# Two of the four chunks of the first layer's feed-forward output as seven products for eight

## The chip, the cores and the metric

The kernel runs on one core of a Trainium2 chip. The metric is the device time of one execution in microseconds, lower is better. TensorE (PE) multiplies, VectorE (DVE) and ScalarE (ACT) work elementwise, GpSimd (POOL) and SyncE (SP) issue transfers. All data is float32.

## The reference

A stack of two layers over 512 tokens (256 of a context, 256 of a latent stream), followed by a second block. The stage of this case is the end of layer 0, whose last part is a gated feed-forward network. D_MODEL is 1024, D_FF is 2816:

```python
def _swiglu(h, w_in, w_out):
    a, b = jnp.split(h @ w_in, 2, axis=-1)
    return (jax.nn.silu(a) * b) @ w_out

xl = xl + ml[5] * _swiglu(_modulate(_rmsnorm(xl, norm_g[l, 1]), ml[3], ml[4]), w_ffn_in[l], w_ffn_out[l])
xc = xc + mc[5] * _swiglu(_modulate(_rmsnorm(xc, norm_g[l, 1]), mc[3], mc[4]), w_ffn_in[l], w_ffn_out[l])
```

The change concerns the last product, with `w_ffn_out` (2816 x 1024). Beside it `w_ada` is multiplied with a condition vector for later layers.

## The kernel before

Activations stand transposed: features on the 128 partitions, the 512 tokens along a row, context in columns 0 to 255 (part 0), latents in 256 to 511 (part 1). `ffn` (in the tile `branches`) holds the 22 feature tiles between the two feed-forward products, `c.x` (`stream`) the residual stream in 8 tiles. The function `tail_of_all` is one stage of the program, ended by a barrier; each engine has its own list of instructions, and semaphores order them.

**Folded products.** The gates, the branches and most up products of this stage (`folded_product`, L1590) use seven multiplications of blocks for eight. A chunk of 256 output features times pairs of input tiles is seen as 2 x 2 blocks, and the two token halves likewise; VectorE forms four sums of weight blocks (`mix_weights`, L1721 to L1724) and four of token blocks (`mix_tokens`), TensorE runs seven products into four banks, ScalarE copies the first, and VectorE puts the results together (`unfold`, L1737 to L1745). The same bank group is used again two products later.

**Down products.** They are plain (`product`, L1566). `down_steps` lists six steps of (chunk, first part, end part); a chunk is 256 output features, so two banks (`half`). Chunks 0 and 1 are made for both parts at once (512 columns), chunks 2 and 3 for part 0 and then again for part 1, so that the norm of part 0 can begin early. The 22 feature tiles come in three weight transfers (`cuts`) of 8, 8 and 6 tiles into a ring of four slots (`weight_ring`, SP, L1554), each released when its products are done (`slot_used`, `product`). VectorE's `add` (L1779) adds a finished bank to `c.x` and counts `drained`; ScalarE squares (L1872, `squared`), TensorE sums the squares over features with a matrix of ones (`sums`, L1627, two steps behind the products), and `average`, `root`, `scale` and `shift` make the normed input of layer 1. `fetch` (L342) loads that layer's first four `w_in` chunks into the same ring.

**Work between.** `condition(n)` lets VectorE do n tiles of the modulation product: each is one 128x1024 operation (L417) on a 512 KB tile that GpSimd loads (L388) into one of two slots, as soon as VectorE has used the one before in it. VectorE's list is fixed by hand:

```python
for s in range(len(down_steps)):
    if s < 2:
        condition(12 if s == 0 else 9)
    add(down_steps, s, P_DOWN, D_DOWN, B_DOWN, 5 * KT)
```

TensorE's banks for it are `B_DOWN + t` modulo 8, so steps 0 to 3 use four different pairs, and only the steps of part 1 wait for `drained`.

Of the kernel before, what the change touches and what calls it, by code (L numbers as in the profile page):

```python
# [1412 lines left out]
def tail_of_all(c, a, w_in, besides, following):  # L1413
# [37 lines left out]
    folded = merges + feeds  # L1451
# [7 lines left out]
    down_steps = [(0, 0, 2), (1, 0, 2), (2, 0, 1), (3, 0, 1), (2, 1, 2), (3, 1, 2)]  # L1459
# [16 lines left out]
    B_OUT, B_SUMS, B_UP, B_DOWN = 0, KT, KT + 2, 4  # L1476
    B_SUMS_2 = B_DOWN + KT
# [42 lines left out]
    with c.stage() as block:  # L1520
        @block.sync
        def _(sp):
# [5 lines left out]
            def wait_used(n):  # L1528
# [9 lines left out]
                elif n < W_DOWN:  # L1538
                    sp.wait_ge(c.folded_product, 4 * (n - weight_of(len(merges)) + len(merges) + 1))
                else:  # L1540
                    s, _, cut = down[n - W_DOWN]
                    if cut == len(cuts) - 1:
                        sp.wait_ge(c.product, P_DOWN + 2 * (s + 1))
                    else:
                        sp.wait_ge(c.slot_used, s * (len(cuts) - 1) + cut + 1)
# [13 lines left out]
        def _(pe):  # L1559
# [60 lines left out]

            def sums(steps, s, base, i):
# [48 lines left out]
            for n in range(len(merges), len(folded)):  # L1670
                folded_product(n)

            for s, (chunk, p0, p1) in enumerate(down_steps):
                for cut, (k0, nk) in enumerate(cuts):
                    w = weights(W_DOWN + s * len(cuts) + cut)
                    for half in range(2):
                        t = 2 * chunk + half
                        if cut == 0 and p0 == 0:
                            pe.wait_ge(c.folded_read, 4 * (len(folded) - (2 if t < 4 else 1) + 1))
                        elif cut == 0:  # L1680
                            pe.wait_ge(c.drained, D_DOWN + evacuations(down_steps, step_of(down_steps, chunk, 0)))
# [8 lines left out]
                if s:  # L1690
                    sums(down_steps, s - 1, wide * KT, B_SUMS_2)
# [3 lines left out]
        def _(dve):  # L1695
# [7 lines left out]
            def mix_tokens(source, out):  # L1703
# [8 lines left out]
                dve.sem_inc(c.tokens_mixed, 1)  # L1712

# [57 lines left out]
            def add(steps, s, base, first, i, gate_tile):  # L1771

                chunk, p0, p1 = steps[s]
                for half in range(2):
                    t = 2 * chunk + half
                    dve.wait_ge(c.product, base + 2 * s + half + 1)
                    for p in range(p0, p1):
                        out = c.x[:, t, cols(p, p + 1)]
                        dve.scalar_tensor_tensor(out, bank(i + t)[:, cols(p, p + 1)],  # L1779
                                                 mod[:, gate_tile + t, parts[p][2]:parts[p][2] + 1], out, ALU.mult, ALU.add  # L1780
                                                 ).then_inc(c.drained, 1)
# [1757 lines left out]
```

## Time and profile before

| | |
|---|---|
| median of 3 runs | 3318.43 us (3316.75 to 3320.65) |
| the profiled execution | 3313.01 us |
| its span, first to last instruction | 3310.9 us |
| mean granted TensorE clock | 0.985 of full speed |
| TensorE, VectorE, ScalarE busy | 92%, 50%, 23% of the span |

Times in rows are us from the start of the span. In a timeline a row merges like instructions in a row; what stands in brackets is idle time before it and what ended it. A float32 product of the program stands in the trace as two matmul records, so an `x` count of 176 is 88 products.

### The profile page before, as it was taken

What the parts mean: (1) busy time and instruction counts of PE and PEld (TensorE: products, weight loads), DVE (VectorE), ACT (ScalarE), POOL (GpSimd) and SP (SyncE); (2) the same over time, 40 slices, a digit from 0 to 9 for tenths busy, and PEclk for the clock granted to TensorE, in tenths of its full rate; (3) what the DMA queues carried; (4) which work ended last, traced back from release to release, by engine and by line L of the source; (5) the groups of instructions that cost most, each with busy time, mean ns of one, the idle gap of its engine ahead of it and who ended that gap; (6) DMA issues with size and microseconds to landing.
All of it is one profiled execution on the core that took longest, in us unless ns stands there. A gap on an engine that the chain in (4) does not pass through costs nothing. (4 is left out here: it accounts for less than half of the span.)

```text
span 3310.9 us, 33325 instructions
## 1 busy us (share of the span) xinstructions
PE 3061.8 (92%) x12426; PEld 2120.6 (64%) x12426; DVE 1652.8 (50%) x3666; ACT 770.0 (23%) x1787; POOL 337.1 (10%) x371
## 2 busy tenths in 40 slices
PE   6999999999999999998999989999988899877776
PEld 2556555758888888485776678878877754322222
DVE  4333444357773676313234437644037377777774
ACT  2222133321001100012111330010023244444443
POOL 0000000000000000100000000000000044444442
PEclk8999999999999999999999999999989999999999
DMA  6221111134442454642322224478431499999997
GB/s 231 83 66 55 51 51 51 51 120 147 127 134 70 141 159 130 197 143 77 102 77 64 64 77 152 152 274 315 143 118 65 142 417 421 421 421 421 420 418 308
DMA packets 280767, 585.87 MB, mean 177 GB/s; under 512 B 11736, under 2 KB 231768, under 8 KB 244256
## 3 DMA queue, kind: packets, MB, share of 16 engines
q0 software_dynamic: 51936, 343.17, 26.3%
q1 hardware_dynamic: 228672, 240.58, 22.5%
q8 instruction: 100, 1.64, 0.2%
q14 instruction: 59, 0.48, 0.0%
HBM read 582.63 MB, written 1.08 MB: 176 GB/s over the span
## 5 line engine op out<-in xcount | busy, mean ns | idle before, releaser
L773 PE MATMUL banks<-normed,weight_ring 128*128 128x512 f32 (+1 forms) x1280 | 487.6, 536 | 29.7 <-PEq L308 18.4
L773 PEld LDWEIGHTS banks<-normed,weight_ring 128*128 128x128 f32 x1280 | 244.7, 193 | 251.5 <-issue 240.0
L782 PE MATMUL banks<-weight_ring,normed 128*128 128x256 f32 x1408 | 319.3, 383 | 4.6 <-DVE work L1263 4.6
L3365 PE MATMUL banks<-weight_ring,work 128*128 128x512 f32 x512 | 248.1, 612 | 60.1 <-ACT work L3265 59.3
L3365 PE MATMUL banks<-work 128*128 128x512 f32 x512 | 253.6, 618 | 53.6 <-ACT work L3265 49.3
L782 PEld LDWEIGHTS banks<-weight_ring,normed 128*128 128x128 f32 x1408 | 265.4, 191 | 58.9 <-issue 23.9
L417 DVE CUSTOM_DVE_ANT_0 work<-work 128x1024 f32<-128x1024 f32 x188 | 223.2, 1223 | 126.1 <-DMA work<-ada_turned 106.4
L2029 PE MATMUL banks<-normed,weight_ring 128*128 128x256 f32 x1088 | 242.4, 386 | 10.6 <-DMA weight_ring<-w_ffn_in 4.0
L2029 PEld LDWEIGHTS banks<-normed,weight_ring 128*128 128x128 f32 x1088 | 210.8, 194 | 41.6 <-DMA weight_ring<-w_ffn_in 4.8
L3365 PEld LDWEIGHTS banks<-weight_ring,work 128*128 128x128 f32 x512 | 88.8, 189 | 198.9 <-ACT work L3265 134.1
L3365 PEld LDWEIGHTS banks<-work 128*128 128x128 f32 x512 | 88.4, 190 | 198.3 <-ACT work L3265 131.6
L1566 PE MATMUL banks<-branches,weight_ring 128*128 128x256 f32 (+1 forms) x656 | 207.5, 478 | 3.4 <-PEq L308 3.4
L3170 DVE CUSTOM_DVE_ANT_0 work<-work,branches 128x1024 f32<-128x1024 f32 x128 | 156.9, 1225 | 95.5 <-DMA work<-experts,branches 94.1
L3170 DVE CUSTOM_DVE_ANT_0 weight_ring<-weight_ring,branches 128x1024 f32<-128x1024 f32 x128 | 156.7, 1225 | 89.8 <-DMA weight_ring<-experts,branches 88.8
L1566 PEld LDWEIGHTS banks<-branches,weight_ring 128*128 128x128 f32 x656 | 124.6, 190 | 84.6 <-issue 75.5
L1590 PE MATMUL banks<-work 128*128 128x256 f32 x744 | 165.6, 379 | 0.0
L3147 POOL DMA_INDIRECT weight_ring<-experts,branches x128 | 141.6, 1107 | 180.6 <-PE banks L3365 174.3
L2029 PE MATMUL banks<-branches,weight_ring 128*128 128x256 f32 x736 | 159.8, 379 | 0.0
L3147 POOL DMA_INDIRECT work<-experts,branches x128 | 134.7, 1053 | 244.0 <-PE banks L3365 170.6
L1590 PEld LDWEIGHTS banks<-work 128*128 128x128 f32 x744 | 141.4, 190 | 19.2
L2029 PEld LDWEIGHTS banks<-branches,weight_ring 128*128 128x128 f32 x736 | 139.8, 190 | 19.0
L1289 DVE TENSOR_REDUCE work<-banks 128x2 f32<-128x1024 f32 (+1 forms) x48 | 50.2, 1046 | 200.3 <-PE banks L885 200.3
(492 smaller groups left out, 3920.4 us busy)
## 6 DMA issues: line engine op xcount, KB each, us to landing
weight_ring<-w_in SPq DMA_DIRECT2D x98, 1024.0 KB, 5.2
weight_ring<-w_ffn_in SPq DMA_DIRECT2D x44, 1024.0 KB, 5.2
work<-ada_turned POOLq DMA_DIRECT2D x80, 512.0 KB, 3.8
work<-ada_turned POOLq DMA_DIRECT2D x18, 1536.0 KB, 9.7
weight_ring<-w_ffn_out SPq DMA_DIRECT2D x20, 1024.0 KB, 5.2
weight_ring<-w_out SPq DMA_DIRECT2D x12, 1024.0 KB, 5.1
weight_ring<-w_br_ml SPq DMA_DIRECT2D x8, 1024.0 KB, 5.1
weight_ring<-w_br_da SPq DMA_DIRECT2D x8, 1024.0 KB, 5.2
```

The lines of the kernel that those rows point to most:

```text
L417: last = dve.tensor_tensor_reduce(out=out, in0=slot[:, t, :], in1=self.rows[:, row, :], scale=1.0, scalar=0.0, op0=ALU.mult, op1=ALU.add, ...
L773: last = pe.matmul(proj_bank(tile)[:, since:T], w[:, kk, half * P:(half + 1) * P], c.h[:, kk, since:T], start=kk == 0, stop=kk == KT - 1)
L782: last = pe.matmul(proj_bank(tile)[:, x * CHUNK:(x + 1) * CHUNK], c.h[:, kk, j * P:(j + 1) * P], w[:, kk, :], start=kk == 0, stop=kk == KT ...
L1289: chain(dve.reduce_max(its[:, 6:8], c.psum[:, u:u + 2, 0:keys(i)], AX.X))
L1566: ins = pe.matmul(bank(i)[:, cols(p0, p1)], w[:, k - at, half * P:(half + 1) * P], source[:, k, cols(p0, p1)], start=k == 0, stop=k == tot ...
L1590: last = pe.matmul(out[:, half * NCTX:(half + 1) * NCTX], left(k), right(k), start=k == 0, stop=k == KT // 2 - 1)
L2029: ins = pe.matmul(bank(i)[:, 0:NLAT], w[:, k - at, half * P:(half + 1) * P], source[:, k, lat], start=k == 0, stop=k == total - 1)
L3147: pool.indirect_dma_start(out=fetched[e % R], out_offset=None, in_=a["experts"], in_offset=bass.IndirectOffsetOnAxis(ap=experts_u[:, e:e + ...
L3170: dve.tensor_tensor_reduce(out=urows[e % R], in0=urows[e % R], in1=tokens[:, t, :], scale=1.0, scalar=0.0, op0=ALU.mult, op1=ALU.add, accu ...
L3365: last = pe.matmul(c.banks[2 * t + half][:], diag[:, r, :], vrows[r][:, half * 512:(half + 1) * 512], start=e == t * H * K, stop=e == (t + ...
```

## The change

Chunks 1 and 2 of the down product become folded, over both parts at once. `down_steps` has five steps: chunk 0, chunks 1 and 2 (both folded), chunk 3 part 0, chunk 3 part 1. A folded step (`folded_down`) runs seven products of 11 tile pairs with 256 columns. Its weight sums are formed for each of the three transfers (`mix_down`) and wait in `down_sums`; all three transfers must be in the ring before the step's first product. The sums of the features (`mix_features`) are made for the 11 pairs of `ffn`: four pairs inside the loop of up products, seven behind it. `add_down` replaces `add`; the squares of steps 0 and 1 go to other tiles, and their sums by TensorE are made behind step 3. Step 0 uses banks 6 and 7, step 1 banks 4 to 7, step 2 banks 0 to 3.

```diff
+    downs = [("down", 0, 1), ("down", 0, 2)]
+    folded = merges + feeds + downs
+    FIRST_DOWN = len(merges) + len(feeds)
...
-    down_steps = [(0, 0, 2), (1, 0, 2), (2, 0, 1), (3, 0, 1), (2, 1, 2), (3, 1, 2)]
+    down_steps = [(0, 0, 2), (1, 0, 2), (2, 0, 2), (3, 0, 1), (3, 1, 2)]
+    mixed_features = ([c.mg[:, 2 * i:2 * i + 2, :] for i in range(4)] + [c.h[:, 2 * i:2 * i + 2, :] for i in range(4)]
+                      + [token_sums[:, i] for i in range(3)])
+    mixed_features = [(v if i >= 8 else v.rearrange("p a (b t) -> p (a b) t", b=2)) for i, v in enumerate(mixed_features)]
+    last_sums = [c.work[:, SUMS_AT + 3072:SUMS_AT + 3840], c.big[:, 22:24, :].rearrange("p k t -> p (k t)")[:, 0:768]]
+    down_sums = [[weight_sums[:, i, x] for x in range(4)] for i in range(2)]
+    down_sums.append([last_sums[x // 2].rearrange("p (s k m) -> p s k m", s=2, m=P)[:, x % 2] for x in range(4)])
+    held_squares = {0: gates[1].rearrange("p (k t) -> p k t", t=T), 1: gates[0].rearrange("p (k t) -> p k t", t=T)}
+    def squares_of(step, t, down):
+        return held_squares[step][:, t % 2] if down and step in held_squares else c.h[:, t]
+    def down_bank(t, part):
+        return (6 + t) if t < 2 else (4 + t % 2 - 4 * part)
...
                     s, _, cut = down[n - W_DOWN]
-                    if cut == len(cuts) - 1:
-                        sp.wait_ge(c.product, P_DOWN + 2 * (s + 1))
+                    if s in (1, 2):
+                        sp.wait_ge(c.weights_mixed, FIRST_DOWN + s)
+                        sp.wait_ge(c.slot_used, s + 2)
+                    elif cut == len(cuts) - 1:
+                        sp.wait_ge(c.product, P_DOWN + 2 * (s + 1 if s == 0 else s - 1))
                     else:
-                        sp.wait_ge(c.slot_used, s * (len(cuts) - 1) + cut + 1)
+                        sp.wait_ge(c.slot_used, cut + 1 + (2 * s - 2 if s else 0))
...
+            def folded_down(s):
+                n, chunk = FIRST_DOWN + s - 1, s
+                slots = [weights(W_DOWN + s * len(cuts) + cut) for cut in range(len(cuts))]
+                first, second, third, fourth = (c.banks[4 * (n % 2) + i] for i in range(4))
+                def their(inputs, outputs):
+                    return lambda k: part_of(slots[k // 4], inputs, outputs)[:, k % 4]
+                def mixture(i):
+                    return lambda k: down_sums[k // 4][i][:, k % 4]
+                def tokens(inputs, half):
+                    return lambda k: quarter(ffn, 2 * k + inputs, half)
+                def token_mixture(i):
+                    return lambda k: mixed_features[k][:, i]
+                def one(out, half, left, right):
+                    for k in range(NF // 2):
+                        last = pe.matmul(out[:, half * NCTX:(half + 1) * NCTX], left(k), right(k), start=k == 0, stop=k == NF // 2 - 1)
+                    return last
+                pe.wait_ge(c.folded_copied, n - 1)
+                one(first, 0, their(0, 0), tokens(0, 0)).then_inc(c.folded_product, 1)
+                pe.wait_ge(c.folded_read, 4 * (n - 2) + 4)
+                one(second, 0, their(1, 0), tokens(1, 0))
+                pe.wait_ge(c.tokens_mixed, 9)
+                if s == 1:
+                    pe.wait_ge(c.drained, D_DOWN + evacuations(down_steps, 0))
+                one(fourth, 1, their(1, 1), token_mixture(3)).then_inc(c.slot_used, 1)
+                pe.wait_ge(c.weights_mixed, n + 1)
+                one(second, 1, mixture(1), token_mixture(1)).then_inc(c.folded_product, 1)
+                one(third, 0, mixture(0), token_mixture(0))
+                one(third, 1, mixture(2), token_mixture(2)).then_inc(c.folded_product, 1)
+                one(fourth, 0, mixture(3), tokens(1, 1)).then_inc(c.folded_product, 1)
...
                 chunk, p0, p1 = steps[s]
                 pe.wait_ge(c.squared, base + evacuations(steps, s))
                 for p in range(p0, p1):
                     for t in (2 * chunk, 2 * chunk + 1):
-                        ins = pe.matmul(bank(i + p)[:, cols(p, p + 1)], c.constant("ones"), c.h[:, t, cols(p, p + 1)],
-                                        start=t == 0, stop=t == KT - 1)
+                        ins = pe.matmul(bank(i + p)[:, cols(p, p + 1)], c.constant("ones"),
+                                        squares_of(s, t, steps is down_steps)[:, cols(p, p + 1)], start=t == 0, stop=t == KT - 1)
...
             for s, (chunk, p0, p1) in enumerate(down_steps):
+                if s in (1, 2):
+                    folded_down(s)
+                    continue
                 for cut, (k0, nk) in enumerate(cuts):
                     w = weights(W_DOWN + s * len(cuts) + cut)
                     for half in range(2):
                         t = 2 * chunk + half
-                        if cut == 0 and p0 == 0:
-                            pe.wait_ge(c.folded_read, 4 * (len(folded) - (2 if t < 4 else 1) + 1))
-                        elif cut == 0:
-                            pe.wait_ge(c.drained, D_DOWN + evacuations(down_steps, step_of(down_steps, chunk, 0)))
+                        if cut == 0:
+                            pe.wait_ge(c.folded_read, 4 * (FIRST_DOWN - 1 if s == 0 else FIRST_DOWN + s - 2))
                         for k in range(k0, k0 + nk):
                             if s == 0 and half == 0 and k % 2 == 0:
                                 pe.wait_ge(c.fed, k // 2 + 1)
-                            last = product(B_DOWN + t, w, half, ffn, p0, p1, (k,), k0, NF)
+                            last = product(down_bank(t, p0), w, half, ffn, p0, p1, (k,), k0, NF)
                         if cut == len(cuts) - 1:
                             last.then_inc(c.product, 1)
                     if cut < len(cuts) - 1:
                         last.then_inc(c.slot_used, 1)
-                if s:
-                    sums(down_steps, s - 1, wide * KT, B_SUMS_2)
+                    if s == 4 and cut == 0:
+                        sums(down_steps, 3, wide * KT, B_SUMS_2)
+                if s == 3:
+                    pe.wait_ge(c.folded_read, 4 * len(folded))
+                    for done in range(3):
+                        sums(down_steps, done, wide * KT, B_SUMS_2)
             sums(down_steps, len(down_steps) - 1, wide * KT, B_SUMS_2)
...
+            def mix_features(pairs):
+                for i in pairs:
+                    out, b = mixed_features[i], ffn[:, 2 * i:2 * i + 2, :].rearrange("p two (h t) -> p two h t", h=2)
+                    chain(dve.tensor_tensor(out[:, 0], b[:, 0, 1], b[:, 0, 0], ALU.subtract))
+                    chain.mark(dve.tensor_tensor(out[:, 2], b[:, 1, 1], b[:, 0, 1], ALU.subtract))
+                    chain(dve.tensor_tensor(out[:, 1], b[:, 1, 1], out[:, 0], ALU.subtract))
+                    chain.mark(dve.tensor_tensor(out[:, 3], b[:, 1, 0], out[:, 1], ALU.subtract))
+                chain.wait()
+                dve.sem_inc(c.tokens_mixed, 1)
+            def mix_down(s, cut):
+                n, (_, nk) = W_DOWN + s * len(cuts) + cut, cuts[cut]
+                wait_weights(dve, n)
+                w = c.ring[:, n % SLOTS, 0:nk, :]
+                if s == 2:
+                    dve.wait_ge(c.folded_product, 4 * (FIRST_DOWN + 1))
+                out = down_sums[cut]
+                chain.mark(dve.tensor_tensor(out[0], part_of(w, 0, 1), part_of(w, 1, 1), ALU.add))
+                chain(dve.tensor_tensor(out[2], part_of(w, 0, 0), part_of(w, 0, 1), ALU.subtract))
+                chain(dve.tensor_tensor(out[1], out[0], part_of(w, 0, 0), ALU.subtract))
+                chain(dve.tensor_tensor(out[3], part_of(w, 1, 0), out[1], ALU.subtract))
+                if cut == len(cuts) - 1:
+                    dve.sem_inc(c.weights_mixed, 1)
...
+            def add_down(s):
+                chunk, p0, p1 = down_steps[s]
+                if s in (1, 2):
+                    unfold(FIRST_DOWN + s - 1)
+                    dve.wait_ge(c.folded_read, 4 * (FIRST_DOWN + s))
+                for half in range(2):
+                    t = 2 * chunk + half
+                    if s not in (1, 2):
+                        dve.wait_ge(c.product, P_DOWN + 2 * (s if s == 0 else s - 2) + half + 1)
+                    for p in range(p0, p1):
+                        out = c.x[:, t, cols(p, p + 1)]
+                        source = spare.rearrange("p (k t) -> p k t", t=T)[:, half] if s in (1, 2) else c.banks[down_bank(t, p0)]
+                        dve.scalar_tensor_tensor(out, source[:, cols(p, p + 1)], mod[:, 5 * KT + t, p:p + 1], out, ALU.mult, ALU.add
...
-            for n in range(len(merges), len(folded)):
+            for n in range(len(merges), FIRST_DOWN):
                 _, i, chunk = folded[n]
-                if n + 1 < len(folded):
+                if n + 1 < FIRST_DOWN:
                     mix_weights(n + 1)
+                if i and 1 <= chunk <= 4:
+                    mix_features((chunk - 1,))
                 condition(2 if i == 0 else 1)
                 unfold(n)
                 if i:
                     feed(n, chunk)
             scales(mod_next, KT, c.vector("norm_g", 2 * KT, 3 * KT))
-            for s in range(len(down_steps)):
-                if s < 2:
-                    condition(12 if s == 0 else 9)
-                add(down_steps, s, P_DOWN, D_DOWN, B_DOWN, 5 * KT)
-                if s == len(down_steps) - 2:
-                    average(0, 3, B_SUMS_2)
-                    scale(0, 3)
+            dve.wait_ge(c.folded_product, 4 * FIRST_DOWN)
+            mix_features(range(4, NF // 2))
+            condition(12)
+            for cut in range(2):
+                mix_down(1, cut)
+            add_down(0)
+            mix_down(1, 2)
+            condition(9)
+            add_down(1)
+            for cut in range(3):
+                mix_down(2, cut)
+            for s in (2, 3):
+                add_down(s)
+            average(0, 3, B_SUMS_2)
+            scale(0, 3)
+            add_down(4)
...
             for s in range(len(down_steps)):
+                if s in (1, 2):
+                    copy_first(FIRST_DOWN + s - 1)
```

TensorE at steps 0 and 1, before: the last rows of step 0 (chunk 0), all of step 1 (chunk 1, from the row that waits for `loaded1` on), and the first sums.

```order
L1566 MATMUL banks<-branches,weight_ring 128x512 [waits fed]
L1566 MATMUL banks<-branches,weight_ring 128x512 x7
L1566 MATMUL banks<-branches,weight_ring 128x512 [waits folded_read,loaded1]
L1566 MATMUL banks<-branches,weight_ring 128x512 x7
L1566 MATMUL banks<-branches,weight_ring 128x512 [waits folded_read]
L1566 MATMUL banks<-branches,weight_ring 128x512 x7
L1566 MATMUL banks<-branches,weight_ring 128x512 [waits loaded2]
L1566 MATMUL banks<-branches,weight_ring 128x512 x15
L1566 MATMUL banks<-branches,weight_ring 128x512 [waits loaded3]
L1566 MATMUL banks<-branches,weight_ring 128x512 x11
L1627 MATMUL banks<-normed,constants_sb 128x256 [waits squared]
```

After the change, step 1 from its first product to the fourth:

```order
L1661 MATMUL banks<-branches,weight_ring 128x256 [waits loaded3,folded_copied,loaded2,loaded1]
L1661 MATMUL banks<-branches,weight_ring 128x256 x10
L1661 MATMUL banks<-branches,weight_ring 128x256 [waits folded_read]
L1661 MATMUL banks<-branches,weight_ring 128x256 x10
L1661 MATMUL banks<-merged,weight_ring 128x256 [waits drained,tokens_mixed]
L1661 MATMUL banks<-merged,weight_ring 128x256 x3
L1661 MATMUL banks<-normed,weight_ring 128x256 x4
L1661 MATMUL banks<-work,weight_ring 128x256 x3
L1661 MATMUL banks<-merged,work 128x256 [waits weights_mixed]
L1661 MATMUL banks<-merged,work 128x256 x3
```

The plain step of 44 products waited for weights and for free banks that had been read long before. The folded step waits ahead of its third product (22 products in) for `drained`, the adds of step 0, and for the sums of the features, and 11 products later for the sums of its own weights.

VectorE ahead of the first `add`, before: the last of the 12 tiles, the four adds of step 0, and the first of the 9 tiles.

```order
L417 ISA work,modulation<-work 128x1024 [waits ada_summed,ada_loaded0]
L417 ISA modulation 128x1
L1779 SCALAR_TENSOR_TENSOR stream<-banks,modulation,stream 128x256 [waits ada_summed,product]
L1779 SCALAR_TENSOR_TENSOR stream<-banks,modulation,stream 128x256
L1779 SCALAR_TENSOR_TENSOR stream<-banks,modulation,stream 128x256 [waits product]
L1779 SCALAR_TENSOR_TENSOR stream<-banks,modulation,stream 128x256
L417 ISA work,modulation<-work 128x1024 [waits ada_summed,ada_loaded1]
L417 ISA modulation 128x1
```

After the change, from the last of the 12 tiles on (L1795 to L1798 are `mix_down`, L1884 is `add_down`):

```order
L417 ISA work,modulation<-work 128x1024 [waits ada_summed,ada_loaded0]
L417 ISA modulation 128x1
L1795 TENSOR_TENSOR work<-weight_ring 128x512 [waits ada_summed,loaded1]
L1796 TENSOR_TENSOR work<-weight_ring 128x512
L1797 TENSOR_TENSOR work<-work,weight_ring 128x512 [waits vec_done]
L1798 TENSOR_TENSOR work<-weight_ring,work 128x512 [waits vec_done]
L1795 TENSOR_TENSOR work<-weight_ring 128x512 [waits loaded2,vec_done]
L1796 TENSOR_TENSOR work<-weight_ring 128x512
L1797 TENSOR_TENSOR work<-work,weight_ring 128x512 [waits vec_done]
L1798 TENSOR_TENSOR work<-weight_ring,work 128x512 [waits vec_done]
L1884 SCALAR_TENSOR_TENSOR stream<-banks,modulation,stream 128x256 [waits product,vec_done]
L1884 SCALAR_TENSOR_TENSOR stream<-banks,modulation,stream 128x256
```

The twelve tiles, in front of these rows in both, are now behind 28 operations of `mix_features`, of which these are the last pair's, with the first tile:

```order
L1780 TENSOR_TENSOR work<-branches 128x256
L1781 TENSOR_TENSOR work<-branches 128x256 [waits vec_done]
L1782 TENSOR_TENSOR work<-branches,work 128x256
L1783 TENSOR_TENSOR work<-branches,work 128x256 [waits vec_done]
L417 ISA work,modulation<-work 128x1024 [waits vec_done,ada_summed,ada_loaded1]
L417 ISA modulation 128x1
```

Before, only the two operations of `scales` stood between the end of the feed and the first tile. And eight operations on weights now stand between the last of the 12 tiles and the adds that TensorE waits for.

## Rows read from the trace of the kernel before

**Rows 1.** The page: span, busy time, share and instructions of two engines.

```profile
span 3310.9 us, 33325 instructions
...
PE 3061.8 (92%) x12426; PEld 2120.6 (64%) x12426; DVE 1652.8 (50%) x3666; ACT 770.0 (23%) x1787; POOL 337.1 (10%) x371
```

**Rows 2.** Busy time in a stretch: engines, granted clock, DMA share, GB/s.

```profile
1345.00:1360.00 15.00, 15.00 (x36) 6.65 (x35) 6.16 (x10) 0.00 (x0) 2.13 (x5) 1.00 0.76 243
```

**Rows 3.** Timeline of TensorE, 1320 to 1491: start, length, instruction, count.

```profile
1320.12 3.62 PE L1590 MATMUL banks<-normed,weight_ring 128*128 128x256 f32 x16
...
1332.20 75.70 PE L1566 MATMUL banks<-branches,weight_ring 128*128 128x512 f32 x176
1407.74 1.89 PE L1627 MATMUL banks<-normed,constants_sb 128*128 128x256 f32 x8
1409.46 19.16 PE L1566 MATMUL banks<-branches,weight_ring 128*128 128x256 f32 x88
1428.46 1.89 PE L1627 MATMUL banks<-normed,constants_sb 128*128 128x256 f32 x8
...
1488.89 1.03 PE L1627 MATMUL banks<-normed,constants_sb 128*128 128x256 f32 x4
1490.08 1.13 PE L1627 MATMUL banks<-normed,constants_sb 128*128 128x256 f32 x4 [0.16 <-ACT normed L1872]
```

**Rows 4.** Timeline of VectorE, 1334 to 1370.

```profile
1334.79 1.22 DVE L417 CUSTOM_DVE_ANT_0 work<-work 128x1024 f32<-128x1024 f32 x1
...
1340.12 1.23 DVE L417 CUSTOM_DVE_ANT_0 work<-work 128x1024 f32<-128x1024 f32 x1 [2.61 <-DMA work<-ada_turned]
...
1345.37 1.22 DVE L417 CUSTOM_DVE_ANT_0 work<-work 128x1024 f32<-128x1024 f32 x1 [1.76 <-DMA work<-ada_turned]
...
1353.05 1.23 DVE L417 CUSTOM_DVE_ANT_0 work<-work 128x1024 f32<-128x1024 f32 x1 [4.08 <-DMA work<-ada_turned]
...
1367.64 1.23 DVE L417 CUSTOM_DVE_ANT_0 work<-work 128x1024 f32<-128x1024 f32 x1 [0.77 <-DMA work<-ada_turned]
...
1369.03 0.88 DVE L1779 SCALAR_TENSOR_TENSOR stream<-banks,modulation,stream 128x256 f32<-128x256 f32 x2 [0.16 <-DVE modulation L417]
```

**Rows 5.** Timeline of VectorE, 1213 to 1221, then a group of all 256-wide ones.

```profile
1213.52 0.69 DVE L1721 TENSOR_TENSOR work<-weight_ring 128x512 f32<-128x512 f32 x1
1214.13 0.69 DVE L1722 TENSOR_TENSOR work<-weight_ring 128x512 f32<-128x512 f32 x1
1214.85 0.69 DVE L1723 TENSOR_TENSOR work<-work,weight_ring 128x512 f32<-128x512 f32 x1
1215.58 0.69 DVE L1724 TENSOR_TENSOR work<-weight_ring,work 128x512 f32<-128x512 f32 x1
...
1217.97 0.69 DVE L1737 TENSOR_TENSOR work<-first_product,banks 128x512 f32<-128x512 f32 x1 [0.21 <-DVE modulation L417]
1220.17 0.69 DVE L1740 TENSOR_TENSOR work<-work,banks 128x512 f32<-128x512 f32 x1 [1.52 <-PE banks L1590]
...
L1742 DVE TENSOR_TENSOR work<-work,banks 128x256 f32<-128x256 f32 x31 | 13.0, 421 | 1.1
```

**Rows 6.** SP's issues of weights, and their landing times (min/median/max).

```profile
1346.13 0.37 SPq L1554 DMA_DIRECT2D weight_ring<-w_ffn_out  x1
...
1469.23 20.22 SPq L342 DMA_DIRECT2D weight_ring<-w_in  x4
...
DMA to landing us min/median/max: 4.4/5.3/8.0
```

**Rows 7.** TensorE behind the stage's end, its clock there, and warm.

```profile
1499.03 15.82 PE L773 MATMUL banks<-normed,weight_ring 128*128 128x512 f32 x32 [7.82 <-PEq L308]
...
1499.00:1503.00 4.00, 3.97 (x5) 1.80 (x6) 1.32 (x4) 0.00 (x0) 0.00 (x0) 0.53 0.18 16
...
1571.70 7.03 PE L773 MATMUL banks<-normed,weight_ring 128*128 128x512 f32 x16
```

More of the change, by code:

```diff
@@ L1450, in tail_of_all @@
     feeds = [("up", 0, chunk) for chunk in range(WAVE // 2, NF // 2)] + [("up", 1, chunk) for chunk in range(NF // 2)]
-    folded = merges + feeds
+    downs = [("down", 0, 1), ("down", 0, 2)]
+    folded = merges + feeds + downs
+    FIRST_DOWN = len(merges) + len(feeds)
     gate_number = {}
@@ L1475, in tail_of_all @@
     D_DOWN = wide * KT
-    B_OUT, B_SUMS, B_UP, B_DOWN = 0, KT, KT + 2, 4
-    B_SUMS_2 = B_DOWN + KT
+    B_OUT, B_SUMS, B_UP, B_SUMS_2 = 0, KT, KT + 2, 2
     def weight_of(n):
@@ L1769, in feed, with add @@
                 dve.wait_ge(c.fed, chunk + 1)
-            def add(steps, s, base, first, i, gate_tile):
+            def add(steps, s, base, i, gate_tile):
                 chunk, p0, p1 = steps[s]
@@ L1780, in add @@
                                                  mod[:, gate_tile + t, parts[p][2]:parts[p][2] + 1], out, ALU.mult, ALU.add
+                                                 ).then_inc(c.drained, 1)
+            def add_down(s):
[11 more added lines that the diff above has]
+                        dve.scalar_tensor_tensor(out, source[:, cols(p, p + 1)], mod[:, 5 * KT + t, p:p + 1], out, ALU.mult, ALU.add
                                                  ).then_inc(c.drained, 1)
@@ L1823, in _ @@
             for s in range(len(out_steps)):
-                add(out_steps, s, P_OUT, 0, B_OUT, 2 * KT)
+                add(out_steps, s, P_OUT, B_OUT, 2 * KT)
                 if s == after_context:
@@ L1832, in _ @@
             mix_weights(len(merges))
-            for n in range(len(merges), len(folded)):
+            for n in range(len(merges), FIRST_DOWN):
                 _, i, chunk = folded[n]
-                if n + 1 < len(folded):
+                if n + 1 < FIRST_DOWN:
                     mix_weights(n + 1)
+                if i and 1 <= chunk <= 4:
+                    mix_features((chunk - 1,))
                 condition(2 if i == 0 else 1)
@@ L1864, in squares @@
             def squares(steps, s, first):
+                down = steps is down_steps
                 chunk, p0, p1 = steps[s]
@@ L1871, in squares @@
                         act.wait_ge(c.drained, n)
-                        act.activation(c.h[:, t, cols(p, p + 1)], c.x[:, t, cols(p, p + 1)], ACT.Square).then_inc(c.squared, 1)
+                        act.activation(squares_of(s, t, down)[:, cols(p, p + 1)], c.x[:, t, cols(p, p + 1)], ACT.Square
+                                       ).then_inc(c.squared, 1)
             def root(p, done):
@@ L1905, in _ @@
                 act.activation(ffn[:, j, :], bank(B_UP + j), ACT.Silu).then_inc(c.cleared, 1)
-            for n in range(len(merges), len(folded)):
+            for n in range(len(merges), FIRST_DOWN):
                 copy_first(n)
```

## The prediction

> **What bounds the kernel now.** I read the page first: TensorE is busy for 92% of the span and VectorE for 50% [rows 1]. That average says little of one stage, so I went to the stretch in which the first layer's feed-forward output is made (the down products). TensorE is busy in all of it, at a granted clock of 1.00 [rows 2]. In order of time [rows 3] the last folded product starts at 1320.12, the first down product at 1332.20, and the last down product ends where the sums start, at 1488.89: 156.7 us without a gap. TensorE alone sets the length of this stretch. VectorE is early or late here at no cost: it works through tiles of `condition`, 12 ahead of the first `add` and 9 ahead of the second, and waits for their transfers [rows 4]. Its first `add` starts at 1369.03, just as step 0's products end (1370.0, half of the row of 176).
>
> **What the change takes from TensorE.** A 128x512 product stands as two records: 88 products in 176 records take 1407.74 - 1332.20 = 75.54 us, 0.858 us a product, 37.77 us a chunk of both parts. At 256 columns, 88 records (44 products) take 1428.46 - 1409.46 = 19.0 us, 0.432 each (the step ends with the 1.73 us of sums of the row of 8, so 20.7 to the next). The folded product of before, 28 products of 256 columns (four rows of the timeline with 56 records, of which the first stands here), takes 1332.20 - 1320.12 = 12.08 us, 0.431 each: a folded form pays nothing extra per product [rows 3]. One folded down chunk is 7 x 11 = 77 such products, 33.24 us. Chunk 1 saves 37.77 - 33.24 = 4.53, chunk 2 saves 2 x 19.0 - 33.24 = 4.76. Against it, the sums of step 3 (0.86, the row of 4) now lie inside step 4; before, the corresponding sums (1488.89) filled a wait for the last squares (they run to 1489.75, the last sums start at 1490.08). The other sums, 12 products or 5.2 us, are moved behind step 3 and cost what they cost before. So TensorE's own work up to the last down product falls by 4.53 + 4.76 - 0.86 = 8.4 us. If nobody waited, that were 0.25%.
>
> **What it adds to VectorE, ahead of the feed's end.** Four pairs are mixed in the loop of folded up products. A 128x256 operation lasts 0.42 us, a 128x512 one 0.69; at 512 the next starts 0.61 us later without a wait and 0.72 with one [rows 5]. Less 256 columns (0.27) that is 0.34 and 0.45, so a pair (two of each) takes 1.6 us. It comes behind the weights' sums, which TensorE waits for, and ahead of `condition` and `unfold`. `unfold` starts at 1217.97 now and its second operation waits until 1220.17; it would start at 1219.6 and delay that second one by 0.1 to 0.2 us, with a bank that is wanted 12 us later. Cost nothing; without that cover it would be 4 x 1.6 = 6.4 us.
>
> **Behind it: the first new wait.** Now 7 pairs (7 x 1.6 = 11.2 us) stand ahead of the 12 tiles, which so begin at 1334.8 + 11.2 = 1346.0. The tiles took 34.1 us (1334.79 to 1368.9). Two slots take turns: a slot's next use comes 5.3 us later (1334.79, 1340.12, 1345.37), but 7.7 us later when a weight transfer was issued in between (1345.37 to 1353.05, SP's at 1346.13) [rows 4, 6]. Two such transfers lay in the 34.1 us; moved by 11.2 us, a third does (SP's, when step 0 ends at 1370.0). I take 34.1 + 2.2 = 36.3 us: end at 1382.3. During the 11.2 us no slot is used, so nothing is gained for later tiles beyond the two that are loaded. Then the sums of two weight transfers, 8 operations in 2 x 2.8 us (3 starts of 0.61, 0.72, 0.73 and an end), then `add_down(0)`, 4 operations at 0.44 us (2 take 0.88): it ends at 1382.3 + 5.6 + 1.8 = 1389.7.
>
> TensorE in step 1: 1370.0, first product of 11, 1374.7, second, 1379.5. The next writes bank 7, which step 0 filled, so it waits on `drained` for all of `add_down(0)`: 1379.5 to 1389.7, **10.2 us idle where there was none.** Queued behind it are the other five of step 1's seven products, and with them the release of three ring slots: SP issues three transfers at one go then. What hid the late `add` before was two free pairs of banks.
>
> After it TensorE's clock is low for a while: behind 7.82 us of idle, 32 records took 15.82 us from 1499.03, at a granted clock of 0.53, where 16 of the same take 7.03 later, so 32 at most 14.06 [rows 7]. That is some 2 us. The Trainium skill, TensorE: Matmul & The Clock Gate, Part 1, says that idleness puts the clock to 1.2 GHz and sustained work gives 2.4 GHz back; by that rule the first wait costs 12.2 us and not 10.2, and the trace agrees at 1499.03.
>
> **The second new wait.** Both sides count from the end of `add_down(0)`, call it t. TensorE: 5 products of 11 (23.75) end step 1, three more (14.25) reach the wait for step 2's weight sums, 2 us of low clock: t + 40.0. VectorE: sums of the third transfer (384 wide: 2.3), 9 tiles, `unfold` (2.6: three of 0.72 and one of 0.45), 4 adds (1.8), sums of three transfers (2.8 + 2.8 + 2.3). The 9 tiles start with both slots full: four turns of 5.35 and one tile with its end, 23.0 us. But the burst of three transfers (2.75 MB) falls on them. One transfer alone cost 2.2 us per turn; the burst keeps the engines occupied for one and a half to two turns and more, so between 2.2 and 3 x 2.2 = 6.6; I take 4.5, the middle. So t + 2.3 + 27.5 + 2.6 + 1.8 + 7.9 = t + 42.1: TensorE waits 2.1 us more, and VectorE sets the time.
>
> The rule of the Trainium skill for that burst, DMA: Bandwidth & Descriptors, Queues, rings and completion order, is that each engine takes turns packet by packet between the queues. By it a tile's transfer goes at half rate but never behind the whole burst, as an estimate some 2.6 us longer per turn for as long as it lasts, and the tiles would take 27 to 28 us; if they stood behind it, 30. The row at 1353.05 fits turns.
>
> **The sum.** From t + 42.1: 4 products of 11 (19.0), step 3 (19.0), sums (5.2), step 4 with its sums (19.85): t + 105.15 = 1494.9, against 1488.9. **6.0 us later.** The last sums, the norm and the barrier follow as before (TensorE starts again 10.1 us after 1488.89). The four `w_in` transfers, before from 1469.23 on, now all wait for step 4's last product, since SP asks for slot 0 first; the first has 10.1 us and lands in 5.3 (8.0 at most) [rows 6], so it costs nothing; without that cover up to 5 us. In step 3 and 4 weights come 7 us and more ahead. The profiled execution of before took 3313.01 us with a span of 3310.9, 5.4 under the median 3318.43; the median moves by the same: 3324.4.
>
> **Bounds.** First wait: 8.0 (tiles no slower than 34.1) to 12.5. Burst: tiles 23.0 to 29.6, so the second step from TensorE's t + 40.0 (no wait) to t + 44.2. Together +1.7 to +10.5. A mixed pair has a bound below of 4 x 0.27 = 1.1 us (no overhead) and above of 4 x 0.45 = 1.8: -3.5 and +1.4 on the 7.
>
> **Rivals.** About 6.6 us (0.2%) is what a measurement tells from none.
> (a) Forecast, VectorE late at both places: +1 to +10, chance 0.72; 0.42 of it below 6.6, 0.30 above.
> (b) The second wait is long (burst serves the tiles last, 30 us and more) and the clock falls again: +8 to +14, 0.13. Against it: one transfer costs one turn 2.3 us, not more.
> (c) VectorE is not late, TensorE keeps its 8.4 us: -8.4. It needs 12 tiles in under 26 us, 2.2 us a tile where 2.8 were taken without the third transfer; decided at `add_down(0)` ending before 1379.5. Only if the tiles' transfers go faster. 0.05.
> (d) Waits and savings cancel, 0 to -6.6: total waiting of 2 to 8 us, if the pairs and tiles overlap better than I count. 0.08.
> (e) The late `w_in` burst delays the next stage's gate weights and product by 1 to 5 us on top: 0.02, since the gate product is wanted 15 us into that stage.
> Faster: 0.05. Same: 0.42 + 0.08 = 0.50. Slower: 0.30 + 0.13 + 0.02 = 0.45. The range from 3317 to 3332 leaves out (c), most of the top of (b) and little of (d).
>
> **What would show it.** Folded down chunks of 33.2 us of TensorE work; twelve tiles from about 1346 to 1382; an idle of TensorE of about 10 us behind the second of the seven products of step 1, put down to the adds on `stream`, and clock 0.5 behind it; a second idle of about 2 us before the mixed products of step 2, put down to VectorE's sums of `weight_ring`; the last down product ending near 1495. It is wrong if TensorE has no idle in step 1, if the tiles keep a pace of 2.2 us, or if an idle appears in the folded up products.

## The result and the profile after

The changed kernel takes 3328.47 us in the median of 22 runs, the kernel before 3318.83 us beside it: a ratio of 1.0028, 95% interval 1.0018 to 1.0038. That is 9.3 us slower (6.0 to 12.6). The time lies in the range and on the side of the forecast, whose 6.0 us are the lower end of this interval.

The profiled execution of the change has a span of 3328.0 us. What the change is answerable for is read in the stretch from the first down product to the next stage's first product, called the stretch below. It holds the down products, their sums and the last norm. Before it ran from 1332.20 to 1499.03, 166.83 us [rows 3, 7]. TensorE's timeline after (start, length, instruction, count, idle before):

```profile
1338.57 37.93 PE L1586 MATMUL banks<-branches,weight_ring 128*128 128x512 f32 x88
1376.34 9.66 PE L1661 MATMUL banks<-branches,weight_ring 128*128 128x256 f32 x44
1394.63 3.75 PE L1661 MATMUL banks<-merged,weight_ring 128*128 128x256 f32 x8 [8.63 <-DVE stream L1884]
...
1401.93 1.89 PE L1661 MATMUL banks<-merged,work 128*128 128x256 f32 x8
...
1420.92 9.66 PE L1661 MATMUL banks<-branches,weight_ring 128*128 128x256 f32 x44
...
1439.03 1.99 PE L1661 MATMUL banks<-merged,work 128*128 128x256 f32 x8 [3.70 <-DVEq L1800]
...
1512.30 15.66 PE L773 MATMUL banks<-normed,weight_ring 128*128 128x512 f32 x32 [7.82 <-PEq L308]
```

The stretch now takes 1512.30 - 1338.57 = 173.73 us, 6.9 more. Two idles stand where the down products ran without a gap: 8.63 us, ended by VectorE's adds to `stream` (L1884), and 3.70 us, ended on VectorE's side at the end of its sums of `weight_ring` (L1800). Between 1394.63 and 1401.93 one product of 11 (22 records) takes 7.3 us, where 11 take 4.75 otherwise (44 records in 9.5): 2.55 us of low clock (the lower of its two levels, 1.2 GHz and not 2.4). 8.63 + 3.70 + 2.55 = 14.9 us of loss against 8.4 of saving leaves 6.5. The rest lies at the ends of the idles: a record of this timeline overlaps the next by 0.16 us, and no such overlap is left where one ends before an idle. The clock in the windows of the first idle and behind it (behind the window's length stand busy time and count of TensorE, its weight loads, VectorE, ScalarE and GpSimd; the last three figures are granted clock, DMA share and GB/s):

```profile
1386.00:1394.00 8.00, 0.00 (x0) 0.00 (x0) 7.65 (x13) 0.65 (x2) 1.04 (x2) 0.71 0.44 131
1394.00:1402.00 8.00, 7.37 (x23) 6.12 (x24) 5.00 (x10) 1.21 (x4) 1.06 (x2) 0.65 0.26 71
1402.00:1421.00 19.00, 19.00 (x90) 16.73 (x89) 6.17 (x10) 0.00 (x0) 2.11 (x4) 1.00 0.89 288
```

VectorE is busy for 7.65 of the 8.00 us in which TensorE does nothing: it finishes the last tile and makes the weight sums and the adds. Its timeline, from the end of the seven pairs on:

```profile
1352.64 1.23 DVE L417 CUSTOM_DVE_ANT_0 work<-work 128x1024 f32<-128x1024 f32 x1 [0.25 <-DVE work L1783]
...
1385.89 1.23 DVE L417 CUSTOM_DVE_ANT_0 work<-work 128x1024 f32<-128x1024 f32 x1 [0.25 <-DVE modulation L417]
...
1392.83 1.66 DVE L1884 SCALAR_TENSOR_TENSOR stream<-banks,modulation,stream 128x256 f32<-128x256 f32 x4
...
1396.86 1.23 DVE L417 CUSTOM_DVE_ANT_0 work<-work 128x1024 f32<-128x1024 f32 x1 [0.25 <-DVE branches L1798]
...
1412.57 1.23 DVE L417 CUSTOM_DVE_ANT_0 work<-work 128x1024 f32<-128x1024 f32 x1 [6.40 <-DMA work<-ada_turned]
...
1438.36 0.56 DVE L1798 TENSOR_TENSOR branches<-weight_ring,work 128x384 f32<-128x384 f32 x1
```

Twelve tiles from 1352.64 to 1387.1, sums, adds until 1394.5, nine tiles from 1396.86, and the last weight sum ends at 1438.9, where TensorE resumes at 1439.03.

The remaining 10 us between the two profiled spans can't be put down to the change. TensorE reached the stretch 6.4 us later (1338.57 against 1332.20), in a part whose instructions differ only by four pairs of feature sums, and a second profile of either kernel (below) reached it at 1332.76 (changed) and 1334.31 (before), so the sign turns. The other 3.8 us lie behind the stretch, where the instructions are the same; no run here looks for their cause. In all comparisons of the whole, hence, the interval counts and not the pair of profiles.

### The profile page after: what moved, and what is told of

Same layout as the page of the kernel before. It is cut to its first block and busy times, and to the rows that moved or that the text cites. A ratio compares the mean times of both kernels' runs of the same rounds, so it can differ in the third digit from the quotient of the medians.

```text
span 3328.0 us, 33517 instructions
## 1 busy us (share of the span) xinstructions
PE 3068.4 (92%) x12470; PEld 2136.8 (64%) x12470; DVE 1690.1 (51%) x3742; ACT 770.0 (23%) x1789; POOL 334.6 (10%) x371
## 5 line engine op out<-in xcount | busy, mean ns | idle before, releaser
L773 PE MATMUL banks<-normed,weight_ring 128*128 128x512 f32 (+1 forms) x1280 | 490.3, 539 | 29.7 <-PEq L308 18.4
L2148 PEld LDWEIGHTS banks<-branches,weight_ring 128*128 128x128 f32 x736 | 139.8, 190 | 19.0
L1586 PE MATMUL banks<-branches,weight_ring 128*128 128x512 f32 (+1 forms) x392 | 133.0, 501 | 3.4 <-PEq L308 3.4
L388 POOL DMA_DIRECT2D work<-ada_turned x98 | 51.8, 529 | 788.8 <-DVEq L423 788.8
```

The lines of the kernel that those rows point to most:

```text
L388: pool.dma_start(self.slots[n % ADA_SLOTS][:, 0:nt, :], self.a["ada_turned"][which, :, t0:t0 + nt, :]).then_inc(c.ada_loaded[n % ADA_SLOTS ...
L773: last = pe.matmul(proj_bank(tile)[:, since:T], w[:, kk, half * P:(half + 1) * P], c.h[:, kk, since:T], start=kk == 0, stop=kk == KT - 1)
L1586: ins = pe.matmul(bank(i)[:, cols(p0, p1)], w[:, k - at, half * P:(half + 1) * P], source[:, k, cols(p0, p1)], start=k == 0, stop=k == tot ...
L2148: ins = pe.matmul(bank(i)[:, 0:NLAT], w[:, k - at, half * P:(half + 1) * P], source[:, k, lat], start=k == 0, stop=k == total - 1)
```

## The experiments

The stretch is read from one profile each. In the ratios, which the table at the end of this section collects, the whole kernel is compared with runs of before on the same chip.

**Tiles spread.** The same instructions, the tiles in other places:

```diff
             mix_features(range(4, NF // 2))
-            condition(12)
+            condition(6)
             for cut in range(2):
                 mix_down(1, cut)
             add_down(0)
             mix_down(1, 2)
-            condition(9)
+            condition(8)
             add_down(1)
             for cut in range(3):
                 mix_down(2, cut)
+            condition(7)
             for s in (2, 3):
                 add_down(s)
```

> The 21 condition tiles stand as 6, 8 and 7 (behind the sums of step 2) instead of 12 and 9. The stretch is counted from the first down product to the next stage's first product: 166.8 us before the change, 173.7 after it. Theory 1, VectorE's list makes add_down(0) and the weight sums late and nothing else costs: the add ends before TensorE's third product of step 1, no idle over 1 us in the stretch, stretch 158.4 us (8.4 under before), whole kernel 0.25% faster than before and 15 us faster than the change. Theory 2, the folded form itself pays for its banks, three ring slots and transfers in a burst: an idle of 3 us or more stays in step 1 or 2, stretch above 161. Theory 3, half of the loss lies outside this stretch: stretch 158.4, but the whole kernel within 5 us of before.

Theory 1 holds, in the stretch to the tenth of a microsecond. TensorE:

```profile
1335.47 37.93 PE L1586 MATMUL banks<-branches,weight_ring 128*128 128x512 f32 x88
1373.23 9.66 PE L1661 MATMUL banks<-branches,weight_ring 128*128 128x256 f32 x44
...
1406.47 9.66 PE L1661 MATMUL banks<-branches,weight_ring 128*128 128x256 f32 x44
...
1439.71 19.16 PE L1586 MATMUL banks<-branches,weight_ring 128*128 128x256 f32 x88
...
1493.88 16.57 PE L773 MATMUL banks<-normed,weight_ring 128*128 128x512 f32 x32 [7.82 <-PEq L308]
```

Each folded step takes 33.24 us, as worked out, and no down product waits: 1493.88 - 1335.47 = 158.41 us, 8.4 under before. The adds that TensorE waited for are where they are wanted, at the end of step 0 (its first half's adds at 1371.22, the second's wait 1.34 us for the product). They end at 1374.3, and TensorE's third product starts at 1382.73:

```profile
1371.22 0.88 DVE L1884 SCALAR_TENSOR_TENSOR stream<-banks,modulation,stream 128x256 f32<-128x256 f32 x2
1373.43 0.88 DVE L1884 SCALAR_TENSOR_TENSOR stream<-banks,modulation,stream 128x256 f32<-128x256 f32 x2 [1.34 <-PE banks L1586]
...
1396.80 1.22 DVE L417 CUSTOM_DVE_ANT_0 work<-work 128x1024 f32<-128x1024 f32 x1 [5.43 <-DMA work<-ada_turned]
```

The burst of three transfers is still there: a tile waits 5.43 us in it, and nobody waits for that tile. The whole kernel: 0.9966 (0.9952 to 0.9980), 11.3 us faster than before (6.6 to 15.9), which holds the 8.4. Theory 2 falls, since no idle of 3 us stays, and theory 3, since the whole gains more than 5 us.

**Tiles later.** `condition(6)` ahead of the first sums and `condition(15)` in place of `condition(9)`.

> The tiles stand as 6 and 15: the first add early, six more tiles ahead of the second. Theory 1: the first idle of 8.6 us goes, and the second grows from 3.7 to about 18 to 20 us, since 15 tiles at 3.2 us, unfold, adds and sums (12.4 us) start at about 42 us into the stretch and TensorE wants the sums at 85: stretch about 158.4 + 19 + 2 = 179 us, slower than the change. Rival, the first idle alone is the loss and the second is a wait for transfers: stretch 158.4 + 3.7 = 162 us.

The first idle is gone and the second is 12.70 us, with the low clock behind it (8 records in 3.78 us where they take 1.89 otherwise):

```profile
1434.32 3.78 PE L1661 MATMUL banks<-merged,work 128*128 128x256 f32 x8 [12.70 <-DVEq L1800]
```

The stretch takes 1509.50 - 1336.20 = 173.3 us, 6 less than I expected: the fifteen tiles took 44.6 us (1377.42 to 1422.0), 3.0 a tile and not 3.2, and the wait I had set 1 to 3 us high beside that. The mechanism stands, and the rival (162) doesn't: what is gained at the adds of step 0 is paid at the weight sums of step 2.

**Add first.** `add_down(0)` ahead of all three `mix_down(1, cut)`, the tiles as in the change.

> add_down(0) stands ahead of all sums of step 1's weights instead of behind two thirds of them. Theory, VectorE's list as a whole sets the time: the first idle falls by 5.6 us to about 3 to 5, a new idle of up to 3 us appears before the products that want the weight sums, and the second idle at step 2 grows by what was won, to about 7 to 9, since the nine tiles start at the same time: stretch 173 to 174 us, as the change. Rival, each wait is a loss of its own: stretch 173.7 - 5.6 = 168 us, or less if the low clock goes too.

```profile
1381.64 3.41 PE L1661 MATMUL banks<-merged,weight_ring 128*128 128x256 f32 x8 [3.36 <-DVE stream L1884]
...
1389.29 1.99 PE L1661 MATMUL banks<-merged,work 128*128 128x256 f32 x8 [0.97 <-DVEq L1800]
...
1428.66 3.78 PE L1661 MATMUL banks<-merged,work 128*128 128x256 f32 x8 [5.86 <-DVEq L1800]
```

Three idles of 3.36, 0.97 and 5.86 us and a stretch of 1504.15 - 1330.86 = 173.3 us. Counted from the start of the stretch, TensorE starts again 5.3 us earlier than in the change (at 50.8 us for 56.1) and at step 2 only 2.7 us earlier (97.8 for 100.5). Those 2.7 us are the nine tiles, which took 26.8 us here and 29.7 there; the rest of VectorE's list came out where it did. The low clock behind the 5.86 us, which the change's profile doesn't have at that place, cost 2.2 us. So the rival's 168 us is out, and the end of VectorE's list, not the length of a single wait, sets when TensorE goes on. That the whole stretch comes within 0.4 us of the change is in part chance: a quick draw of tiles and a fall of the clock cancel. The last idle of 5.86 us is short of the 7 to 9 I expected for the same reason.

**Last three tiles later.** `condition(12)` stays, `condition(9)` becomes `condition(6)`, and the last 3 tiles stand behind the sums of step 2.

> The tiles stand as 12, 6 and 3 (behind the sums of step 2). The first idle stays near 9 to 10 us with about 2.5 us of low clock behind it, the second one goes: stretch 158.4 + 9 to 10 + 2.5 = 170 to 171 us. If the low clock is no loss of its own because VectorE is late anyway, 167.5 to 168.5.

```profile
1393.32 3.75 PE L1661 MATMUL banks<-merged,weight_ring 128*128 128x256 f32 x8 [9.59 <-DVE stream L1884]
```

The second idle goes; the first is 9.59 us, with 2.2 us of low clock behind it; stretch 1506.62 - 1336.30 = 170.3 us. Here the low clock is a loss of its own: 158.4 + 9.6 + 2.2 = 170.2. In the change it was hidden in VectorE's lateness, as the forecast had it.

**All features behind.** No `mix_features` in the loop of up products, `range(0, NF // 2)` behind it.

> All 11 pairs of feature sums stand behind the feed, none in the loop of folded up products. If the four in the loop were free, as forecast: the loop is as before (12.09 us a product), the twelve tiles start 6.4 us later, the first idle grows from 8.6 to 15.0, and the stretch from 173.7 to about 180. If the pairs in the loop cost TensorE time too: the loop shortens by the same, and the whole is even.

First idle 14.32 us, second 3.37, and the stretch 1521.68 - 1339.13 = 182.55 us, 8.8 over the change. TensorE comes out of the second wait 5.9 us later, close to the 6.4 that were added, and 2.9 us more are lost since the clock fell behind that wait as well (8 records in 3.78 us), which it did not behind the 3.70 us of the first profile. The whole: 1.0042 (1.0020 to 1.0063). The loop takes 12.09 us a product with the four pairs in it and without them, so there they were free.

**Burst of two.** Step 3's first weights wait for the end of step 1's products:

```diff
                     if s in (1, 2):
                         sp.wait_ge(c.weights_mixed, FIRST_DOWN + s)
                         sp.wait_ge(c.slot_used, s + 2)
+                        if s == 1 and cut == 2:
+                            sp.wait_ge(c.folded_product, 4 * (FIRST_DOWN + 1))
```

> Only the third transfer of the burst behind step 1's release (step 3's first weights) waits until step 1's products are done. If the burst slows the nine tiles: they take 27 to 28 us instead of 29.7, the second idle shrinks from 3.7 to about 1.5 to 2, stretch 171.5 to 172. If the tiles' pace is the two slots' own turn and not the burst: nine tiles 29 to 30 us, second idle 3.7, stretch 173.7. First idle 8.6 in both.

The nine tiles took 27.1 us (1398.67 to 1425.8) and the second idle was 1.20, both as the first theory says; the first idle was 10.42 and not 8.6, though nothing ahead of it had been touched. But with the whole burst the nine tiles took 27.2 us in the second profile of the change (below) and 26.8 with the add first. The experiment doesn't tell the two theories apart, and it has no ratio for the whole kernel. How much the third transfer costs the tiles stays open.

**w_in early,** in the spread version and in the change:

```diff
-            fetch(c, sp, following, lambda s: wait_used(max(n for n in range(n_all) if n % SLOTS == s)))
+            for s in (1, 2, 3, 0):
+                wait_used(max(n for n in range(n_all) if n % SLOTS == s))
+                sp.dma_start(c.ring[:, s, 0:following[s].shape[1], :], following[s]).then_inc(c.ahead[s], 16)
+                c.ahead_n[s] += 1
+            c.fetched = True
```

> The spread tiles (6, 8, 7) together with the next layer's first w_in transfers in the order of slots 1, 2, 3, 0, so that three of the four leave before step 4 ends. If the late w_in burst costs nothing (forecast): stretch 158.4 us as with the spread tiles alone, the whole the same within the measurement. If it is rival (e): TensorE's first products of the next stage come 1 to 5 us earlier than with the spread tiles alone.

> The change with only the w_in order 1, 2, 3, 0. Gate weights: their copy on VectorE waited 3.9 us at the next stage's start with the change, 1.1 before it; with early transfers it should wait about 1.1 again, and the gate product still not wait in either. Stretch and the first 15 us of the next stage as with the change.

In the spread version the stretch is 1497.34 - 1338.92 = 158.4 us with it and without it, and the whole 0.9969 (0.9956 to 0.9982): rival (e) is out. In the change the copy of the gate weights waits 1.10 us with it and 3.86 without; the product that wants them comes 10 us and more behind the copy and waits in neither. There I had expected the stretch of the change, and it came out at 177.4 us. That isn't the doing of the `w_in` transfers, the first of which leaves at 1479.83: the 3.6 us were lost before 1460.64, where step 3's products start. The idles were 9.51 and 3.70 us, and behind the 3.70 the clock fell this time:

```profile
1438.99 3.78 PE L1665 MATMUL banks<-merged,work 128*128 128x256 f32 x8 [3.70 <-DVEq L1804]
```

**Both kernels once more,** one profile each.

> The changed kernel profiled once more. Theory, idles of 3 to 4 us bring the low clock in some executions only, and the tiles' transfers vary by 1 to 2 us: first idle 8.5 to 10.5, second 1 to 4, the eight records behind the second take either 1.9 or 3.8 us, stretch 172.5 to 177.5, of which 173.7 was one draw. Rival, the stretch is fixed and the rest of the measured difference lies elsewhere: 173.7 within 0.3.

> The kernel before profiled once more. Without idles in the stretch it should be fixed: 166.8 us within 0.2, whatever the whole execution takes. If it varies by over 1 us, differences of stretches can't be read to a microsecond.

The kernel before: 1501.13 - 1334.31 = 166.82 us, the 166.83 of the first profile. The change: 1504.98 - 1332.76 = 172.2 us, idles of 9.64 and 1.60:

```profile
1389.83 3.75 PE L1661 MATMUL banks<-merged,weight_ring 128*128 128x256 f32 x8 [9.64 <-DVE stream L1884]
...
1431.72 1.99 PE L1661 MATMUL banks<-merged,work 128*128 128x256 f32 x8 [1.60 <-DVEq L1800]
```

So the stretch of before is fixed and that of the change is not, which puts out the rival of a fixed 173.7. In the table, "low clock" is what was lost to it behind the first and the second idle, reckoned against the version with tiles 6, 8, 7.

| kernel | first idle | second | low clock | stretch, us | whole, ratio to before |
|---|---|---|---|---|---|
| before, two profiles | none | none | none | 166.8, 166.8 | 1 |
| change, first profile | 8.63 | 3.70 | 2.6, 0 | 173.7 | 1.0028 (1.0018 to 1.0038) |
| change, second profile | 9.64 | 1.60 | 2.1, 0 | 172.2 | as above |
| change, w_in early | 9.51 | 3.70 | 2.8, 2.6 | 177.4 | not timed |
| burst of two | 10.42 | 1.20 | 2.5, 0 | 172.9 | none |
| add first | 3.36 and 0.97 | 5.86 | 1.8, 2.2 | 173.3 | 1.0016 (1.0003 to 1.0029) |
| tiles 6 and 15 | none | 12.70 | 0, 1.9 | 173.3 | 1.0031 (1.0016 to 1.0046) |
| features behind | 14.32 | 3.37 | 3.1, 2.9 | 182.6 | 1.0042 (1.0020 to 1.0063) |
| tiles 12, 6, 3 | 9.59 | none | 2.2, 0 | 170.3 | 1.0000 (0.9985 to 1.0015) |
| tiles 6, 8, 7 | none | none | none | 158.4 | 0.9966 (0.9952 to 0.9980) |
| tiles 6, 8, 7, w_in early | none | none | none | 158.4 | 0.9969 (0.9956 to 0.9982) |

The difference of stretches lies in the interval of the whole for every version that was timed (for the last two -8.4 us in -6.6 to -15.9 and -6.0 to -14.6), but for the second profile of the change, whose 5.4 us are just under 6.0 to 12.6. The intervals are 7 to 14 us wide, so this agreement is a weak one.

## Why the prediction was right

**TensorE's saving.** 8.4 us forecast, 8.4 measured once nobody waited. The price of a product at 256 columns carried over to 11 in a row, and the sums behind step 3 cost what they did.

**Pairs of features.** 11.2 us for seven pairs forecast; 1341.16 to 1352.4, 11.2 measured. Those in the loop were free.

**The first wait.** 10.2 us forecast, 8.6 measured (8.6 to 10.4 over the profiles that keep this order). The term that was too large is the twelve tiles: 36.3 us against 34.5. The third weight transfer that I added for 2.2 us came (SP issued at 1352.50, 1366.23 and 1376.53), but the twelve tiles took 34.5 us in the first profile of the change, 35.5 in the second and 36.3 (1352.64 to 1388.9) in the burst-of-two run, all with three such transfers beside them. Against the 34.1 of before its price was 0.4 to 2.2 us; what decides it isn't shown.

**The low clock.** 2 us forecast from the next stage's start, 2.55 behind the first idle (2.1 to 3.1 in the other profiles with that idle), and no part of the time of the change, since VectorE was later still. As shown by the version with 12, 6 and 3 tiles, it counts as soon as VectorE is in time.

**The second wait.** 2.1 us forecast, 3.7 measured, at t + 44.5 and not t + 42.1. The term that was too small is the nine tiles: 27.5 us against 29.7, just over the bound of 29.6; in the second profile they took 27.2, and TensorE waited 1.6. Of the two values that the forecast weighed, 27 to 28 us if the tiles' transfers and the burst take turns and 30 if the tiles stand behind it, both occur: 26.8 to 30.0 us in five profiles with the whole burst. The runs don't decide how the two share the engines. What I left out of the number, though rival (b) names it, is that the clock may fall a second time behind a wait so short: of three profiles whose second wait was 3.4 to 3.7 us it did in two, for 2.6 and 2.9 us. So the stretch's cost has a spread of its own, 172.2 to 177.4 us. That this fills the step from 6.9 us to the 9.3 of the medians is an argument and not shown: the interval starts at 6.0.

**Luck in the sum.** The path is the forecast one, but the number is closer than its terms. `add_down(0)` ended 1.6 us earlier in the stretch than forecast, and the wait behind it 2.4 us later; they cancel to 0.8 of the 0.9 us between 6.0 and 6.9.

**Rivals.** By time alone the 9.3 us of the whole lie in (a), 1 to 10, and in (b), 8 to 14, and above the 6.6 us below which I had put the larger half of (a). The profiles tell them apart: two of the change show (a), 5.4 and 6.9 us with no second fall of the clock, and the one with `w_in` early, whose VectorE list is the same, shows (b): nine tiles in 29.9 us, a second fall, 10.5 us. How often either comes isn't measured. (c), no lateness, gave 8.4 us and only in the order that puts six tiles ahead of the first add: the condition given (add_down(0) ending before TensorE's third product) decided it. (d) didn't happen: the waits came to over 11 us in each profile of the change. (e) is out.

## What to carry to other kernels

A saving on the busiest engine of 8.4 us was worth -6.9 (-5.4 in the second profile), since the helper's work for it went in front of a filler (the condition tiles) that had been placed where lateness was free; the same instructions with the filler cut into three pieces gave all 8.4 us. When a change turns a free result into one that is waited for, go through the helper's list and ask for each deadline what stands ahead of it that nobody wants yet. And don't price idles one by one: work out both engines up to the last point where they meet. Moving an add forward by 5.6 us brought TensorE out of its first wait 5.3 us earlier and gained 0.4 us in the stretch.

## What the runs showed of the hardware

The same short idle is followed by the low clock in some executions and not in others. Upstream of the stretch a 2.24 us idle of TensorE occurs at the same place in the program, three times in each execution; in the first profile of the kernel before the 16 records behind it took

```profile
428.07 7.11 PE L773 MATMUL banks<-normed,weight_ring 128*128 128x512 f32 x16 [2.24 <-DVE work L1261]
494.31 7.10 PE L773 MATMUL banks<-normed,weight_ring 128*128 128x512 f32 x16 [2.24 <-DVE work L1261]
560.55 8.80 PE L773 MATMUL banks<-normed,weight_ring 128*128 128x512 f32 x16 [2.24 <-DVE work L1261]
```

and in the first profile of the change

```profile
429.58 8.80 PE L773 MATMUL banks<-normed,weight_ring 128*128 128x512 f32 x16 [2.24 <-DVE work L1261]
497.52 8.80 PE L773 MATMUL banks<-normed,weight_ring 128*128 128x512 f32 x16 [2.24 <-DVE work L1261]
565.46 8.80 PE L773 MATMUL banks<-normed,weight_ring 128*128 128x512 f32 x16 [2.24 <-DVE work L1261]
```

The granted clock at the fast one at 494.31 is 1.00 all through (2.4 GHz); at the slow one at 560.55 it is 0.50 from 562 to 564 (1.2 GHz). One fall of three against three of three, 1.7 us each and 3.4 us together, in code that is the same. It isn't the kernel that decides: the second profile of before has two falls, that of the change one. The 3.4 us are a part of the 6.4 us by which the two first profiles differ ahead of the stretch, and show why two spans are no measure of a change of this size.

Behind the 7.82 us ahead of the next stage the clock was low in each of the twelve profiles: the 32 records there took 15.4 to 16.9 us, against 14.06 at most at full clock. So it was behind each of the longer idles of the stretch, 8.63 to 14.32 us.
